# Eight conditioning products moved from TensorE to VectorE, the expert loop's head placed at a fixed slot, and each next loop bound read inside the body

## The chip, the cores and the metric

The kernel runs on one core of a Trainium2 chip. The metric is the device time of one execution in microseconds (us); lower is better. All arithmetic is fp32.

## The reference, cut to what matters

One layer over x of 256 tokens by 1024 columns, with a conditioning vector c:

```python
mod = silu(c) @ w_ada + b_ada                  # 6 x 1024: shift1, scale1, gate1, shift2, scale2, gate2
h = rms_norm(x, norm1_g) * (1 + scale1) + shift1
z = h @ w_in                                   # inputs of the convolution, q/kv latents, two branch gates
y_conv = zb * short_causal_conv(zc * zx)       # 8 channel tiles of 128
y_mla = mla_branch(...)                        # 8 heads, latent attention, rotary part of 64
x = x + gate1 * ((sig(zg_conv)*y_conv + sig(zg_mla)*y_mla) @ w_o)
h2 = rms_norm(x, norm2_g) * (1 + scale2) + shift2
for each token: top-1 group of 4, then top-2 of its 8 experts:
    out += weight * ((silu(h2 @ w_gate[e]) * (h2 @ w_up[e])) @ w_down[e])
x = x + gate2 * out
```

## The kernel before

Every engine has a queue written out by hand; they meet at counting semaphores. There is no planner.

**Setup and latents.** The columns of `w_ada` come in 12 items of 512 columns (`ada_d[n]`, 2 MB each: 8 row tiles `k` of 128 x 512). An item on TensorE (`ada_item`) is 8 x 4 matmuls: for each row tile `k` and each quarter `q`, silu(c) repeated over 32 columns (`c_rep`) is the stationary operand of column group `q`, and 128 columns of the weights stream past. In fp32 each matmul shows as two records, so an item is 64. Its result, 4 groups of 32 equal rows, is copied by ScalarE (`ada_copied`), transposed (L649, `ada_turned`) and added to the bias by VectorE (L950, `mod_ready`). Items 0 to 3 (shift1, scale1) are needed for the latents and run at the start. They are not touched.

**Heads.** A loop over 8 heads, unrolled, runs attention for head `h` and, woven into it, the convolution's projections for head `h + 1` and item `4 + h` of the modulation. TensorE's order in head `h`: q, k (`qk_ready`), attention output of head `h - 1`, tile 0 of the next head's projection (it waits for that head's weights, `ring_landed`), v (`v_ready`), sums of squares, tiles 1 and 2, scores (`s_ready`), **the item** (`ada_done`), tile 3, the item's transpose, tile 4, transposes of the probabilities. VectorE in head `h`: `q_x`, `q_n`, `merge(h - 1)`, the rotary products in even heads (L917, L919, L920), the reciprocal of the key norm (L922), `k_n`, `k_r`, `conv_taps(h + 1)`, the score maximum, the softmax's scaling, the bias add of the item (L950), `conv_gated(h + 1)` (L892, L893).

**SyncE's queue of transfers.** Weights of the heads go by turns into two slots of a ring (`mix_load`, 3.0 to 3.2 MB). `beside_load(j)` brings item `4 + j` into the head of expert place 3 (`ada_beside`). Experts 0 to 2 are loaded in heads 1 to 3. One queue holds, for each `c`: `mix_load(c + 2)` behind `v_ready` of head `c`, an expert, then `beside_load(c + 1)` behind `ada_done` of item `4 + c`. Experts 3 to 6 come from the end of the heads on.

**Experts.** Tokens are sorted into windows of 32 slots, each of one expert: here 35 windows for 32 experts. An expert's weights are 3 MB; there are 7 places. Expert `e + 7` is loaded into the place of expert `e` once the last window of `e` has finished (`down_ready`, in `next_expert`). TensorE runs an outer loop of 4 rounds over 7 unrolled places, and the last 4 experts unrolled behind it. For each expert an inner loop runs over its windows; its bounds are read from a table in SBUF (`windows_before`, a register load). A window is: gate and up products (32 matmuls), `gather` of the next window's rows (8), a transpose behind `gu_copied` (L770), `combine` (8), `turn_rows` of the next window (L744, L745), the down products (8).

Of the kernel before, what the change touches and what calls it, by code (L numbers as in the profile page):

```python
# [8 lines left out]
ALU = mybir.AluOpType  # L9
# [3 lines left out]
P = 128  # L13
D = 1024
T = 256
KT = D // P
TT = T // P
HEADS = 8
# [7 lines left out]
WIN = 32  # L26
# [44 lines left out]
def block_kernel(nc, xT_d, pos_d, small_d, const_d, ada_d, lat_d, mix_even_d, mix_odd_d, wo_d, ex_d, out_d):  # L71
    with ExitStack() as ctx:
# [3 lines left out]
        def sem(name):  # L76
            return ctx.enter_context(nc.semaphore(name))
# [103 lines left out]

        ada_beside = wex[:, OWN - 1, 0:ADA_COLS]
        ada_rows = wex[:, OWN - 1, GU_COLS:GU_COLS + P]

        def sm(name, i=0, n=None, parts=P):
            a, w = SMALL[name]
# [39 lines left out]
        w_tok_ready, slot_tok_ready, spread_ready, spread_copied = sem("w_tok_ready"), sem("slot_tok_ready"), sem("spread_ready"), sem("spread_copied")  # L226
        y_cleared = sem("y_cleared")
        ada_copied, ada_turned = sem("ada_copied"), sem("ada_turned")
        mod_ready = sem("mod_ready")

        xw_ready, gu_ready, gu_copied, gu_turned = sem("xw_ready"), sem("gu_ready"), sem("gu_copied"), sem("gu_turned")
# [18 lines left out]
        @block.sync  # L250
        def _(sp):
            sp.dma_start(xT[:], xT_d).then_inc(x_landed, 16)
            sp.dma_start(small[:], small_d).then_inc(small_landed, 16)

            def ada_load(n):

                sp.dma_start(wex[:, n, 0:ADA_COLS], ada_d[n]).then_inc(ada_landed[n], 16)  # L257

            def split_load(e, part):
                dst, cols = ((split_head, slice(0, GU_COLS // 2)), (split_tail, slice(GU_COLS // 2, GU_COLS + DOWN_COLS)))[part]  # L260
                sp.dma_start(dst, ex_d[e][:, cols]).then_inc(ex_landed[EX_SLOTS - 1], 16)

            def expert_load(s, e):
                if s < len(ex_place):
                    sp.dma_start(ex_place[s], ex_d[e]).then_inc(ex_landed[s], 16)
                else:
                    split_load(e, 0)
                    split_load(e, 1)

            def ring(n, src):  # L270

                if n == 2:
                    sp.wait_ge(lat_ready, 1)
                elif n > 2:
                    sp.wait_ge(v_ready, n - 2)
                sp.dma_start(ring_slot[n % 2][:, 0:src.shape[1]], src).then_inc(mix_landed[n % 2], 16)

            def mix_load(j):
                ring(MIX0 + j, (mix_even_d, mix_odd_d)[j % 2][j // 2])

            def lat_load(n):
                sp.dma_start(ring_slot[0][:, n * LAT_PART:(n + 1) * LAT_PART], lat_d[n]).then_inc(lat_landed[n], 16)  # L282

            ada_load(0)
            sp.dma_start(const[:], const_d).then_inc(const_landed, 16)
            ada_load(1)
            lat_load(0)
            sp.dma_start(posi, pos_d).then_inc(pos_landed, 16)
            lat_load(1)
            ada_load(2)  # L290
            lat_load(2)
            ada_load(3)
            lat_load(3)
            mix_load(0)

            def beside_load(j):
                sp.wait_ge(ada_done, 4 + j)
                sp.dma_start(ada_beside, ada_d[4 + j]).then_inc(ada_landed[3], 16)

            beside_load(0)  # L300
            mix_load(1)
            for c in range(HEADS):
                if c + 2 < HEADS:
                    mix_load(c + 2)
                else:
                    ring(WO0 + c + 2 - HEADS, wo_d[c + 2 - HEADS])
                if 1 <= c < OWN:
                    expert_load(c - 1, c - 1)
                if c + 1 < HEADS:
                    beside_load(c + 1)  # L310
            sp.wait_ge(ada_turned, 4 + HEADS)
            expert_load(OWN - 1, OWN - 1)
            last = EX_SLOTS - 1
            sp.wait_ge(merged_ready, HEADS)
            split_load(last, 1)
            for n in range(2):
                sp.wait_ge(wo_ready, 2 * n + 2)
                expert_load(OWN + n, OWN + n)
            sp.wait_ge(h2r_ready, 2)
            sp.wait_ge(lg_ready, 1)  # L320
            split_load(last, 0)
            sp.wait_ge(table_ready, 1)

            def next_expert(s, e):

                upto = windows_before(sp, e + 1)
                sp.wait_ge(down_ready, upto)
                expert_load(s, e + EX_SLOTS)

            for e in range(EXPERTS - EX_SLOTS):  # L330
                next_expert(e % EX_SLOTS, e)
            for m in range(KT):
                sp.wait_ge(out_done, m + 1)
                sp.dma_start(out_d[m], xT[:, m, :]).then_inc(out_stored, 16)
            sp.wait_ge(out_stored, 16 * KT)
# [138 lines left out]
        def _(pe):  # L474
# [3 lines left out]
            def ada_item(items, out):  # L478

                w = items.rearrange("p (k c) -> p k c", k=KT)  # L480
                for k in range(KT):
                    for q in range(4):
                        last = mm(out[q * WIN:(q + 1) * WIN, :], c_rep[:, k, :], w[:, k, q * P:(q + 1) * P], k == 0, k == KT - 1)
                return last
# [96 lines left out]
            for h in range(HEADS):  # L581
# [57 lines left out]
                mm(ps[:, 3, P:P + T], q_n[:, P:T], k_n, True, False)  # L639
                mm(ps[:, 3, P:P + T], q_r[rope, P:T], k_r[rope, :], False, True).then_inc(s_ready, 1)  # L640

                pe.wait_ge(ada_landed[3], 16 * h + 32)
                ada_item(ada_beside, ps[:, 0, 0:P]).then_inc(ada_done, 1)
                if h + 1 < HEADS:
                    conv_tile(h + 1, 3, ps[:, 6, T:2 * T]).then_inc(zbg_ready, 1)
                else:
# [86 lines left out]
            def gather(n):  # L733

                pe.wait_ge(sel_ready, n + 1)
                for t in range(TT):
                    for q in range(4):
                        last = mm(ps[q * WIN:(q + 1) * WIN, 3, 0:T], sel[:, t, :], h2_rows[:, t, q * T:(q + 1) * T], t == 0, t == TT - 1)
                last.then_inc(rows_ready, 1)
# [14 lines left out]
                                  False, True, skip_group_check=True)  # L754
                last.then_inc(combined, 1)

            def window(place, use, n):

                wdn = place_down(place).rearrange("p (f c) -> p f c", f=2)

                pe.wait_ge(ex_landed[place], use * (16 if place < len(ex_place) else 32))
                pe.wait_ge(xw_ready, n + 1)
                for k in range(KT):
                    for q in range(4):
                        last = mm(ps[q * WIN:(q + 1) * WIN, 0, 0:P], xw[:, k, :], place_gu(place, k)[:, q * P:(q + 1) * P], k == 0, k == KT - 1)
                last.then_inc(gu_ready, 1)
                gather(n + 1)

                pe.wait_ge(gu_copied, n + 1)
                nc.tensor.transpose(ps[:, 1, 0:P], gu_sb, ident).then_inc(gu_turned, 1)  # L770
                combine(n)
                turn_rows(n + 1)

                pe.wait_ge(act_done, n + 1)
                for f in range(2):
                    for q in range(4):
                        last = mm(ps[q * WIN:(q + 1) * WIN, 2, 0:T], act_t[:, f * WIN:(f + 1) * WIN], wdn[:, f, q * T:(q + 1) * T], f == 0, f == 1)
                last.then_inc(down_ready, 1)

            gather(0)  # L780
            spread(1, slot_tok)
# [1 line left out]
            pe.wait_ge(spread_copied, 2)  # L783
            pe.wait_ge(table_ready, 1)
            ROUNDS = EXPERTS // EX_SLOTS
            with pe.Fori(0, ROUNDS) as i:
                upto = windows_before(pe, i * EX_SLOTS)
                for s in range(EX_SLOTS):
                    at, upto = upto, windows_before(pe, i * EX_SLOTS + (s + 1))
                    with pe.Fori(at, upto) as n:  # L790
                        window(s, i + 1, n)
            upto = windows_before(pe, ROUNDS * EX_SLOTS)
            for e in range(ROUNDS * EX_SLOTS, EXPERTS):
                at, upto = upto, windows_before(pe, e + 1)
                with pe.Fori(at, upto) as n:
                    window(e % EX_SLOTS, ROUNDS + 1, n)
            combine(upto)


        @block.vector  # L800
        def _(dve):
# [93 lines left out]
            def merge(h):  # L895
# [4 lines left out]
                link(v.scalar_tensor_tensor(o_t, m_gate, 1.0, ps[:, 2, T:2 * T], ALU.add, ALU.mult))  # L900
                v.scalar_tensor_tensor(merged[:, h, :], o_t, 0.5, merged[:, h, :], ALU.mult, ALU.add).then_inc(merged_ready, 1)

            conv_taps(0)
            conv_gated(0)
            for h in range(HEADS):
                rope = slice(ROPE * (h % 2), ROPE * (h % 2 + 1))
                dve.wait_ge(sq_ready, h + 1)
# [7 lines left out]
                if h % 2 == 0:  # L915
                    dve.wait_ge(qx_ready, h // 2 + 1)
                    link(v.tensor_tensor(q_r, q_x, cos_t, ALU.mult))  # L917
                    dve.wait_ge(swap_ready, h // 2 + 1)
                    link(v.tensor_tensor(rope_t, sin_t, ps[:, 1, T:2 * T], ALU.mult))  # L919
                    link(v.tensor_tensor(q_r, q_r, rope_t, ALU.add))  # L920
                dve.wait_ge(rk_sqrt, h + 1)
                link(v.reciprocal(rk, rk_s))  # L922
                link(v.tensor_tensor(k_n, rk, ps[:, 0, T:2 * T], ALU.mult))
# [30 lines left out]
                    v.tensor_tensor(sm("b_router"), sm("b_router"), ps[:, 1, 0:36], ALU.add).then_inc(bias_ready, 1)  # L954
                if h + 1 < HEADS:
                    conv_gated(h + 1)
            merge(HEADS - 1)


# [228 lines left out]
```

## Time and profile before

| | |
|---|---|
| median of 3 runs | 537.12 us (532.66, 537.4, 537.12) |
| profiled execution: time / span | 537.62 us / 535.8 us |
| mean granted TensorE clock | 0.988 |
| busy: TensorE / VectorE / ScalarE / GpSimd | 499.5 / 183.6 / 148.1 / 153.2 us |
| moved by DMA | 161.94 MB, 302 GB/s over the span |

The span runs from the first to the last instruction; the remaining 1.8 us of the execution lie around it. The stages: start and latents to about 70 us, heads to about 307 us, router to about 321 us, experts to about 530 us, then the store.

### The profile page before, as it was taken

To read this page: it belongs to the slowest core of one execution; us is meant where nothing else is said; L and a number is where in the kernel's file an instruction comes from. 1 tells how busy PE (TensorE), PEld (TensorE's weight loads), DVE (VectorE), ACT (ScalarE), POOL (GpSimd) and SP (SyncE) were. 2 spreads that over 40 slices of the span, in tenths; PEclk is the share of its full clock that TensorE was granted. 3 is DMA by queue.
4 is the path that set the end of the run, shared out by engine and by line. 5 is a ranking of instruction groups with operands and counts; after the bars stand their busy time and mean duration, and the time that the engine had idled before them with its cause. 6 is when DMAs were issued, how large, how long until landed. Compare 5 with 4: busy or idle time off the path is not lost.

```text
span 535.8 us, 14859 instructions
## 1 busy us (share of the span) xinstructions
PE 499.5 (93%) x6205; PEld 388.9 (73%) x6206; DVE 183.6 (34%) x559; ACT 148.1 (28%) x276; POOL 153.2 (29%) x195
## 2 busy tenths in 40 slices
PE   4699999999999999999999969998999899899994
PEld 3587888888888888888888736765666566566663
DVE  0721624242524252424241442333233323233333
ACT  3012122322222232313131241323332242233221
POOL 0000010101010101010100005766676676677662
PEclk9989999999999999999999988999999999999999
DMA  8996417394959473624446973979999999999972
GB/s 356 414 435 248 178 32 276 125 428 192 417 222 413 183 270 146 254 122 158 157 158 247 393 302 145 369 309 432 425 431 435 429 428 435 428 429 435 425 329 80
DMA packets 10690, 161.94 MB, mean 302 GB/s; under 512 B 1185, under 2 KB 2465, under 8 KB 3105
## 3 DMA queue, kind: packets, MB, share of 16 engines
q1 hardware_dynamic: 10656, 161.45, 73.3%
q8 instruction: 27, 0.44, 0.3%
q14 instruction: 7, 0.05, 0.0%
HBM read 160.40 MB, written 1.05 MB: 301 GB/s over the span
## 4 chain that ended last, share of the span: by engine, by line
PE 83%; DMA 11%; issue 2%; DVE 1%; ACT 1%; SPq 1%; DVEq 0%; ACTq 0%
PE ps L476 79%; DMA wex<-in_ex 7%; DMA wex<-in_ada 4%; PE ps L744 1%; PE ps L770 1%; PE ps L745 1%; DVE xT L1068 1%; ACT act L449 0%; ACT L452 0%; SPq L282 0%; PE ps L662 0%; PE ps L664 0%; PE ps L663 0%; PE ps L649 0%; SPq L257 0%
## 5 line engine op out<-in xcount | busy, mean ns | idle before, releaser
L476 PE MATMUL ps<-act,wmix 128*128 128x256 f32 x864 | 194.6, 382 | 1.0 <-DVE act L850 1.0
L476 PEld LDWEIGHTS ps<-act,wmix 128*128 128x128 f32 x864 | 161.9, 190 | 24.9 <-issue 3.5
L357 POOL TENSOR_SCALAR work<-trig,work 128x256 f32<-128x256 f32 x70 | 65.0, 938 | 63.4 <-issue 54.2
L476 PE MATMUL ps<-wex,work 128*32 128x128 f32 (+1 forms) x1840 | 70.8, 301 | 11.1 <-issue 9.8
L343 POOL TENSOR_TENSOR work<-work,trig 64x256 f32<-64x256 f32 x8 | 5.8, 719 | 254.5 <-ACT work L410 152.9
L476 PE MATMUL ps<-work 32*128 32x256 f32 (+6 forms) x864 | 72.7, 374 | 0.6 <-ACT work L470 0.6
L476 PEld LDWEIGHTS ps<-wex,work 128*32 128x32 f32 x1840 | 50.3, 111 | 29.0 <-issue 14.3
L476 PEld LDWEIGHTS ps<-work 32*128 32x128 f32 (+3 forms) x864 | 47.5, 168 | 13.3 <-issue 3.3
L476 PE MATMUL ps<-act,work 128*32 128x256 f32 (+1 forms) x704 | 43.5, 367 | 2.5 <-DVE work L1035 1.3
L467 ACT ACT_TABLE_LOAD x35 | 44.9, 1283 | 1.0 <-issue 0.4
L361 POOL TENSOR_TENSOR work<-work,trig 128x512 f32<-128x512 f32 x35 | 44.7, 1277 | 0.0
L364 POOL TENSOR_TENSOR work<-work 128x256 f32<-128x256 f32 x35 | 25.5, 730 | 49.0 <-PE ps L476 49.0
L1053 DVE COPY work<-ps 128x128 f32<-128x128 f32 x35 | 10.2, 292 | 84.3 <-PE ps L476 84.3
L470 ACT COPY work<-ps 128x256 f32<-128x256 f32 x35 | 13.0, 373 | 84.1 <-PE ps L476 84.1
L476 PE MATMUL ps<-wmix,work 128*32 128x128 f32 (+2 forms) x704 | 32.6, 294 | 2.0 <-issue 2.0
L476 PEld LDWEIGHTS ps<-wmix,work 128*32 128x32 f32 (+1 forms) x704 | 25.3, 117 | 8.9 <-DVE work L1061 5.8
L476 PEld LDWEIGHTS ps<-act,work 128*32 128x32 f32 x704 | 22.3, 112 | 10.7 <-DVE work L1061 2.1
L476 PE MATMUL ps<-wex,c_rep 128*32 128x128 f32 x768 | 24.6, 282 | 4.4 <-DMA wex<-in_ada 4.4
L476 PEld LDWEIGHTS ps<-wex,c_rep 128*32 128x32 f32 x768 | 21.2, 113 | 8.2 <-DMA wex<-in_ada 5.0
L1061 DVE TENSOR_TENSOR work<-ps,mod 128x256 f32<-128x256 f32 x35 | 14.9, 425 | 33.9 <-PE ps L745 33.9
L467 ACT ACTIVATE work<-ps 128x64 f32<-128x64 f32 x35 | 7.8, 224 | 58.2 <-PE ps L770 58.2
L476 PE MATMUL ps<-work,wmix 128*128 128x256 f32 x104 | 23.8, 379 | 0.0
(181 smaller groups left out, 422.9 us busy)
## 6 DMA issues: line engine op xcount, KB each, us to landing
wex<-in_ex SPq DMA_DIRECT2D x20, 3072.0 KB, 18.5
wex<-in_ada SPq DMA_DIRECT2D x12, 2048.0 KB, 10.7
wmix<-in_ex SPq DMA_DIRECT2D x8, 3072.0 KB, 20.2
wmix<-in_mix_even SPq DMA_DIRECT2D x4, 3200.0 KB, 10.6
wmix<-in_mix_odd SPq DMA_DIRECT2D x4, 3008.0 KB, 10.8
work<-in_ex SPq DMA_DIRECT2D x4, 2048.0 KB, 19.8
wmix<-in_wo SPq DMA_DIRECT2D x2, 2048.0 KB, 8.2
act<-in_ex SPq DMA_DIRECT2D x4, 1024.0 KB, 16.5
```

What stands on the lines that cost most here:

```text
L343: nc.gpsimd.tensor_tensor(k_sq[0:ROPE, :], k_sq[0:ROPE, :], k_rope_sq[0:ROPE, :], ALU.add).then_inc(sq_joined, 1)
L357: nc.gpsimd.tensor_scalar(comb_both[:, rows], slot_row[:, rows], lane_now, None, ALU.is_equal).then_inc(comb_half, 1)
L361: nc.gpsimd.tensor_tensor(comb_both, comb_both, weight_row, ALU.mult).then_inc(comb_pair, 1)
L364: nc.gpsimd.tensor_tensor(comb, comb_both[:, 0:T], comb_both[:, T:2 * T], ALU.add).then_inc(comb_ready, 1)
L467: nc.scalar.activation(silu_t, ps[:, 1, 0:2 * WIN], ACT.Silu).then_inc(silu_done, 1)
L470: nc.scalar.copy(y_sb, ps[:, 2, 0:T]).then_inc(y_copied, 1)
L476: return nc.tensor.matmul(out, lhsT, rhs, start=start, stop=stop, **kw)
L744: nc.tensor.transpose(ps[:, 0, P:2 * P], rows_sb[:, 0:P], ident)
L745: nc.tensor.transpose(ps[:, 0, 2 * P:3 * P], rows_sb[:, P:T], ident).then_inc(rows_turned, 1)
L770: nc.tensor.transpose(ps[:, 1, 0:P], gu_sb, ident).then_inc(gu_turned, 1)
L1053: v.tensor_copy(gu_sb, ps[:, 0, 0:P]).then_inc(gu_copied, 1)
L1061: v.tensor_tensor(xw_v, xw_ps, shift2, ALU.add).then_inc(xw_ready, 1)
```

## The change

It has three parts.

**VectorE's modulation.** For items 4 to 11, VectorE now forms `ada_sum = sum over k of w[:, k, :] * c[k]` (128 x 512) in 8 instructions, each waiting for the one before: steps 0 to 4 of item `4 + h` right behind `conv_gated(h)`, steps 5 to 7 inside head `h`, behind L917 in even heads and behind `merge(h - 1)` in odd ones. TensorE then needs 4 matmuls (8 records) with a matrix of ones to sum over the partitions. `beside_load(j)` now waits for VectorE's sum of the item before (`ada_summed`) and stands ahead of `mix_load` in SyncE's queue.

**Aligned loop.** The outer expert loop's first instruction is put at slot 0 of a block of instructions.

**Bounds.** The upper bound of the next expert but one is read inside `window`, behind the gather, rather than between two experts. It is read again in each window of an expert.

```diff
+        ada_sum = wex[:, OWN - 1, GU_COLS + P:GU_COLS + P + ADA_TILES * P]
...
             def beside_load(j):
-                sp.wait_ge(ada_done, 4 + j)
+                if j == 0:
+                    sp.wait_ge(ada_done, 4)
+                else:
+                    sp.wait_ge(ada_summed, j)
                 sp.dma_start(ada_beside, ada_d[4 + j]).then_inc(ada_landed[3], 16)
...
             for c in range(HEADS):
+                if c + 1 < HEADS:
+                    beside_load(c + 1)
                 if c + 2 < HEADS:
                     mix_load(c + 2)
...
-                if c + 1 < HEADS:
-                    beside_load(c + 1)
...
-                pe.wait_ge(ada_landed[3], 16 * h + 32)
-                ada_item(ada_beside, ps[:, 0, 0:P]).then_inc(ada_done, 1)
+                pe.wait_ge(ada_summed, h + 1)
+                for q in range(4):
+                    last = mm(ps[q * WIN:(q + 1) * WIN, 0, 0:P], ones[:, 0:WIN], ada_sum[:, q * P:(q + 1) * P], True, True)
+                last.then_inc(ada_done, 1)
...
                 gather(n + 1)
+                later = windows_before(pe, following) if following is not None else None
...
-            with pe.Fori(0, ROUNDS) as i:
-                upto = windows_before(pe, i * EX_SLOTS)
+            with nc.Fori(0, ROUNDS, engines=[pe.engine], head_slot={pe.engine: 0}) as i:
+                at, upto = windows_before(pe, i * EX_SLOTS), windows_before(pe, i * EX_SLOTS + 1)
                 for s in range(EX_SLOTS):
-                    at, upto = upto, windows_before(pe, i * EX_SLOTS + (s + 1))
                     with pe.Fori(at, upto) as n:
-                        window(s, i + 1, n)
+                        later = window(s, i + 1, n, i * EX_SLOTS + (s + 2) if s + 1 < EX_SLOTS else None)
+                    at, upto = upto, later
...
+            def ada_steps(j, steps):
+
+                w = ada_beside.rearrange("p (k c) -> p k c", k=KT)
+                if steps[0] == 0:
+                    dve.wait_ge(ada_landed[3], 16 * j + 32)
+                    dve.wait_ge(ada_done, 4 + j)
+                for k in steps:
+                    if k == 0:
+                        link(v.tensor_scalar(ada_sum, w[:, k, :], c_rep[:, k, 0:1], None, ALU.mult))
+                    elif k < KT - 1:
+                        link(v.scalar_tensor_tensor(ada_sum, w[:, k, :], c_rep[:, k, 0:1], ada_sum, ALU.mult, ALU.add))
+                    else:
+                        v.scalar_tensor_tensor(ada_sum, w[:, k, :], c_rep[:, k, 0:1], ada_sum, ALU.mult, ALU.add).then_inc(ada_summed, 1)
+
             conv_taps(0)
             conv_gated(0)
+            ada_steps(0, range(0, 5))
             for h in range(HEADS):
...
                     link(v.tensor_tensor(q_r, q_x, cos_t, ALU.mult))
+                    ada_steps(h, range(5, KT))
                     dve.wait_ge(swap_ready, h // 2 + 1)
...
+                if h % 2 == 1:
+                    ada_steps(h, range(5, KT))
...
                     conv_gated(h + 1)
+                    ada_steps(h + 1, range(0, 5))
```

## Rows read from the trace of the kernel before

**Rows 1.** The page, part 1: busy us, share of the span, instructions.

```profile
PE 499.5 (93%) x6205; PEld 388.9 (73%) x6206; DVE 183.6 (34%) x559; ACT 148.1 (28%) x276; POOL 153.2 (29%) x195
```

**Rows 2.** The chain of waits in order of time: start us, us, what.

```profile
44.97 48.72 PE ps L476 x284
...
319.32 2.13 issue
...
464.04 35.34 DMA wex<-in_ex
...
522.33 2.82 PE ps L476 x80
```

**Rows 3.** Timeline of TensorE in head 4: start, us, engine, line, shapes, count, [idle before].

```profile
196.60 1.95 PE L476 MATMUL ps<-wex,c_rep 128*32 128x128 f32 x64
...
196.60 1.69 PEld L476 LDWEIGHTS ps<-wex,c_rep 128*32 128x32 f32 x64 [0.33 <-issue]
198.48 3.32 PEld L476 LDWEIGHTS ps<-act,wmix 128*128 128x128 f32 x16 [0.20 <-issue]
```

**Rows 4.** Timeline of VectorE in heads 4 and 5.

```profile
183.72 0.42 DVE L917 TENSOR_TENSOR work<-work,trig 128x256 f32<-128x256 f32 x1
...
187.98 0.42 DVE L919 TENSOR_TENSOR work<-trig,ps 128x256 f32<-128x256 f32 x1 [3.84 <-PE ps L476]
...
208.99 0.48 DVE L912 TENSOR_SCALAR work<-ps,work 128x256 f32<-128x256 f32 x1 [5.44 <-ACT work L407]
...
215.48 1.75 DVE L922 RECIPROCAL work<-work 128x256 f32<-128x256 f32 x1 [4.65 <-ACT work L420]
```

**Rows 5.** VectorE's groups with shapes kept apart: count | busy us, mean ns.

```profile
L886 DVE SCALAR_TENSOR_TENSOR work<-work,small 128x256 f32<-128x256 f32 x8 | 3.9, 484 | 0.3
L885 DVE TENSOR_SCALAR work<-work,small 128x256 f32<-128x256 f32 x8 | 2.8, 353 | 0.3
L838 DVE TENSOR_TENSOR act<-xT,work 128x2048 f32<-128x2048 f32 x1 | 2.3, 2292 | 0.0
```

**Rows 6.** Timeline in heads 4 and 5: a ring load's issue, the next slot's use.

```profile
186.59 0.33 SPq L276 DMA_DIRECT2D wmix<-in_mix_even  x1
...
208.64 3.33 PEld L476 LDWEIGHTS ps<-act,wmix 128*128 128x128 f32 x16
```

**Rows 7.** DMA issues at 186.59 and at 198.61 us: KB, us to landing.

```profile
wmix<-in_mix_even SPq DMA_DIRECT2D x1, 3200.0 KB, 10.7
...
wex<-in_ada SPq DMA_DIRECT2D x1, 2048.0 KB, 7.5
```

**Rows 8.** Timeline of TensorE in the experts.

```profile
339.14 2.82 PE L476 MATMUL ps<-wex,work 128*32 128x256 f32 x80
...
381.47 1.95 PE L476 MATMUL ps<-wex,work 128*32 128x128 f32 x64 [0.22 <-issue]
...
384.22 0.14 PEld L770 LDWEIGHTS ps<-const,work 128*128 128x128 f32 x1 [0.41 <-DVE work L1053]
...
387.21 1.69 PEld L476 LDWEIGHTS ps<-wex,work 128*32 128x32 f32 x64 [0.69 <-DVE work L1061]
...
458.46 1.96 PE L476 MATMUL ps<-wex,work 128*32 128x128 f32 x64 [1.37 <-issue]
```

**Rows 9.** Waits from 328 to 500 us: us in total, times, longest us.

```profile
PE ps L476 <- issue: 10.1, 27, 1.5
...
PE ps L476 <- DMA wex<-in_ex: 1.0, 1, 1.0
```

**Rows 10.** Timeline of SyncE's queue: the first and the last four loads into places 0 to 3.

```profile
328.70 28.30 SPq L265 DMA_DIRECT2D wex<-in_ex  x4
...
464.04 17.59 SPq L265 DMA_DIRECT2D wex<-in_ex  x4
```

**Rows 11.** DMA issues at 356.67 and at 481.30 us: KB, us to landing.

```profile
wex<-in_ex SPq DMA_DIRECT2D x1, 3072.0 KB, 11.0
...
wex<-in_ex SPq DMA_DIRECT2D x1, 3072.0 KB, 40.8
```

More of the change, by code:

```diff
@@ L228, in block_kernel @@
         ada_copied, ada_turned = sem("ada_copied"), sem("ada_turned")
+        ada_summed = sem("ada_summed")
         mod_ready = sem("mod_ready")
@@ L755, in combine, with window @@
                 last.then_inc(combined, 1)
-            def window(place, use, n):
+            def window(place, use, n, following):
                 wdn = place_down(place).rearrange("p (f c) -> p f c", f=2)
@@ L778, in window @@
                 last.then_inc(down_ready, 1)
+                return later
             gather(0)
@@ L785, in _ @@
             ROUNDS = EXPERTS // EX_SLOTS
-            with pe.Fori(0, ROUNDS) as i:
-                upto = windows_before(pe, i * EX_SLOTS)
+            with nc.Fori(0, ROUNDS, engines=[pe.engine], head_slot={pe.engine: 0}) as i:
+                at, upto = windows_before(pe, i * EX_SLOTS), windows_before(pe, i * EX_SLOTS + 1)
                 for s in range(EX_SLOTS):
-                    at, upto = upto, windows_before(pe, i * EX_SLOTS + (s + 1))
                     with pe.Fori(at, upto) as n:
-                        window(s, i + 1, n)
-            upto = windows_before(pe, ROUNDS * EX_SLOTS)
+                        later = window(s, i + 1, n, i * EX_SLOTS + (s + 2) if s + 1 < EX_SLOTS else None)
+                    at, upto = upto, later
+            at, upto = windows_before(pe, ROUNDS * EX_SLOTS), windows_before(pe, ROUNDS * EX_SLOTS + 1)
             for e in range(ROUNDS * EX_SLOTS, EXPERTS):
-                at, upto = upto, windows_before(pe, e + 1)
                 with pe.Fori(at, upto) as n:
-                    window(e % EX_SLOTS, ROUNDS + 1, n)
-            combine(upto)
+                    later = window(e % EX_SLOTS, ROUNDS + 1, n, e + 2 if e + 1 < EXPERTS else None)
+                at, upto = upto, later
+            combine(at)
         @block.vector
```

## The prediction, made before the result was known

> **What bounds the kernel now.** I read the page first: TensorE is busy for 499.5 of 535.8 us [rows 1]. Such a share says neither where it is the limit nor what comes next, so I read the chain of waits in order of time. From 44.97 us through all heads the chain is TensorE's own matmuls, one row behind the other, with no wait for another engine [rows 2]; a microsecond of matmul that leaves a head leaves the whole. Between 307 and 319 us lies the router, small steps on several engines, then 2.13 us in which TensorE waits for nothing that the trace shows, just before the expert loop. In the experts the chain is TensorE again, until it jumps at 499.38 us to a load of 35.34 us [rows 2]: a load that had long been queued. TensorE itself waited only 1.0 us for it [rows 9].
>
> So the experts have two limits almost at the same height. *The load stream.* Four loads into places 0 to 3 are issued from 328.70 to 357.0, the last at 356.67 (the start of the last issue, 0.33 before the end of that row) [rows 10]. That one, of expert 10, meets an idle queue: it takes 11.0 us [rows 11]. The last is issued at 481.30 and lands 40.8 us later, at 522.1 [rows 10, 11]. Between them are 21 landings in 522.1 - 367.7 = 154.4 us, 7.35 us each, with the queue never empty. The last window begins at 522.33 [rows 2]: the end hangs on a stream that starts with the end of expert 3. *TensorE.* One window follows another after 5.74 us, of which 0.22 is idle between two experts [rows 8]; 5.52 of it is work and fixed switches. Between two windows of one expert there is no such gap: the down products and the next gate products run through as 80 records [rows 8].
>
> **VectorE's modulation, on TensorE.** An item's 64 records start at 196.60, and the next weight load starts at 198.48: 1.88 us [rows 3]. The weight loads come 1.69 / 64 = 0.026 us apart, so the 64th matmul starts 1.66 us in and, ending at 1.95, lasts 0.29; the next shape's load begins 0.07 before that end. With 8 records the last starts 7 x 0.026 = 0.18 us in: 0.18 + 0.29 - 0.07 = 0.40 us. The saving is 1.48 us an item, and 8 x 1.48 = 11.8 us. Bounds: in pure proportion 7/8 of 1.88, 1.65 an item, 13.2 in all; or 0.2 us more of unseen gap an item (the row's own 0.20), 1.3, 10.4 in all. The rows show 0.33 us in front of the item's weight loads and 0.20 behind them [rows 3]; the Trainium skill (TensorEngine Tiling (Array Packing), Key Properties) says that a change of tiling mode drains the engine. By a saving in proportion it would be 13.2 us; by that rule the two drains stay, and the trace agrees.
>
> **The same, on VectorE.** A step on 256 columns takes 0.484 us with a scalar and a second tensor, 0.353 with a scalar alone; 2048 columns take 2.29 us, 1.12 ns a column with all overhead [rows 5]. The 256 more columns thus cost at most 0.29: 0.77 and 0.64 us, and about 0.04 for each wait on the step before. Steps 0 to 4 are 0.68 + 4 x 0.81 = 3.9 us, steps 5 to 7 2.4 us. Steps 0 to 4 start where `conv_gated` ends, in front of idle time of 5.44 us in odd heads (208.99), more in even ones [rows 4]: 1.5 us to spare. Steps 5 to 7 stand in front of 3.84 us (even, before L919) and 4.65 us (odd, before L922) [rows 4]: 1.4 and 2.2 to spare. TensorE asks for the sum at 196.6, some 10 us after it is there. I cost all of it at nothing. Without this cover (VectorE at twice the rate per step) an odd head would lose 7.8 - 5.4 = 2.4 us, less what TensorE has queued.
>
> **The same, on SyncE's queue.** `beside_load` now waits for VectorE instead of TensorE and moves ahead of `mix_load` and, in heads 1 to 3, of an expert's load; both stand behind its wait and its 2 MB. In an even head the sum is there at 184.1 + 2.4 = 186.5, when the ring load was issued anyway, 186.59 [rows 4, 6]. Alone the item takes 7.5 us, the ring load 10.7 [rows 7]: 18.2 us even if they overlap in nothing, from 186.6 to 204.8. The slot is used at 208.64 [rows 6], 1.5 us earlier by the shorter head, so 2.3 us remain. The expert behind it is needed only after 300 us. GpSimd's queue does not change. Cost: nothing.
>
> **The bounds of the loop.** Taken out: the 0.22 us gap between two experts [rows 8]. Put in: one register load in each of 35 windows, behind the gather; behind it on TensorE's queue stand L770, `combine` and all that follows, and ScalarE and VectorE wait for L770. Its cover is the 0.41 us in which the weight load of L770 waits anyway [rows 8]. No row shows a load by itself. Where it stands today the weight loads pause for 0.69 us [rows 8], with two branches in it, so a load in the body adds x between 0 and 0.69 - 0.41 = 0.28 us a window. I take 0.15, the middle, since an unknown part of the 0.69 is the loop's. What counts before the stream of loads runs: three changes of expert gone (-0.7) and six windows with x: +0.9; together +0.2 (-0.7 to +1.0). The Trainium skill (DMA: Bandwidth & Descriptors, Latency and other measured facts) puts a floor of about 600 ns under a `tensor_load`; an estimate from it is x = 0.6 - 0.41 = 0.19, 0.2 us more in the time. No run here shows such a load alone.
>
> Later on, TensorE has room. From 321.45 (319.32 + 2.13) to the end of the last window, 522.33 + 5.52 = 527.9, it took 206.4 us for 35 windows [rows 2], of which 10.1 us were such gaps and 1.0 the wait for the load [rows 9]: 195.3 without. Three returns to the loop's head remain, 1.37 against 0.22 us [rows 8]: 3.5 us. So it needs 198.8 + 35x, and the load stream gives it 522.1 + 5.5 - 321.45 = 206.1. As long as x is below 7.3 / 35 = 0.21, the stream decides; at 0.28 TensorE decides and is 2.5 us late.
>
> **The aligned loop.** It adds a jump into the loop. Bound: a return to the head costs 1.15 us more than a plain change of expert [rows 8]. Below nothing: the 2.13 us of the entry [rows 2] could shrink to 1.37, 0.8 less. I take +0.2. Its effect on later rounds falls under the stream of loads.
>
> **The sum.** -11.8 (heads) + 0.2 (first experts) + 0.2 (entry) - 0.1 (the last window can start at the landing, 522.1) = -11.5 from the profiled 537.62: 526.1. The median of the three runs lies 0.5 lower, so 525.6.
>
> **Rivals.** (1) *The load in the body makes TensorE the limit.* x of 0.28 to 0.55 instead of 0.15: at 0.28 +2.5, about 528; at 0.55, 198.8 + 19.3 = 218.1 against 206.1, so 12.0 us and with them the whole gain are gone: 537. For it: nothing shows that TensorE's queue reaches over the load. Against: L770 waits anyway. (2) *VectorE or the ring takes part of the heads' gain back.* If a step took 1.1 us rather than 0.8, steps 0 to 4 would reach past the 5.44 us and `merge`, which v waits for, would slip. At 1.3 us a step the overrun is 1.1 us an odd head, some 4 us: 530. Against it: [rows 4, 5]. (3) *Slower: each window pays the load in full.* If the load does not start before the gather has drained and the queue must fill again behind it, the price is the pause of 0.69 plus the 0.41 that no longer overlaps, 1.1 us: 198.8 + 38.5 = 237.3 against 206.1, +31.2 - 11.8 = +19.4: 556. It decides from x = 0.21, and makes the kernel over 1% slower from 0.70. Against it: branches of the inner loop cost nothing visible [rows 8], so the queue does run ahead. (4) *The parts on the loop do nothing and the entry gets dearer by 1.15:* 527, inside the range.
>
> **How the numbers follow.** The forecast has 0.74 with (4) in it; (1) 0.12; (2) 0.09; (3) 0.05. Low end: -13.2 - 0.7 - 0.8 - 0.2 = -14.9, 522.2, and the runs of the kernel before lie up to 4.5 us under their median, of which I grant 1.5: 520.7. High end: -10.4 + 1.0 + 1.15 + 2.5 = -5.75, 531.4; I go to 530, which takes in most of (2) and the lower part of (1) and leaves the rest out. Over 1% faster is below 531.7: the forecast, (2) and a part of (1), 0.86. Within 1%, 0.09; slower by over 1%, 0.05. A measurement of this kernel tells about 1% from no change.
>
> **What would show it.** Right: 8 records of an item in under 0.5 us; heads over about 12 us earlier; VectorE's 128x512 steps at 0.65 to 0.8 us and no wait of TensorE for them; no 0.22 us gap between experts; TensorE waiting longer for loads than the 1.0 us now; the last landing about 12 us before 522. Wrong: a weight load of L770 later than 0.41 us behind the gather in each window, no wait for loads at the end (TensorE decides), waits for `ring_landed` in the heads, or single returns of over 1 us inside an expert of two windows, from where a block of the aligned loop begins.

## The result, and the profile after

The changed kernel takes 520.49 us (519.96 to 520.67), the kernel before 534.89 in the same comparison (532.52 to 537.4): a ratio of 0.9728, 95% interval 0.9668 to 0.9789. The forecast was 525.6; its range ended at 520.7, 0.2 us above the measured time. The profiled execution has a span of 518.8 us against 535.8. Here and below a time is the median of all runs of a kernel, while ratios and their intervals use its fast runs alone, those within 1.5% of its fastest.

The chain of waits of the changed kernel, in order of time (start us, us, what):

```profile
43.20 47.19 PE ps L481 x228
...
303.75 2.52 issue
306.27 4.44 PE ps L481 x80
...
440.58 42.81 DMA wex<-in_ex
483.51 2.82 PE ps L481 x80
```

Beside [rows 2]: the heads begin 1.8 us earlier (43.20 against 44.97), the expert loop 15.2 us earlier (306.27 against 321.45), and the jump to a load that had long been queued is still there, at 483.39 against 499.38. TensorE's timeline in head 4, beside [rows 3]:

```profile
188.72 0.16 PEld L481 LDWEIGHTS ps<-wex,ones 128*32 128x32 f32 x8 [0.33 <-issue]
188.72 0.43 PE L481 MATMUL ps<-wex,ones 128*32 128x128 f32 x8
...
189.07 3.32 PEld L481 LDWEIGHTS ps<-act,wmix 128*128 128x128 f32 x16 [0.20 <-issue]
```

From the item's first weight load to the next shape's it is 0.35 us instead of 1.88, with the same pauses of 0.33 and 0.20 around it: 1.53 us an item, 12.2 in eight. VectorE's timeline around it, beside [rows 4]:

```profile
193.71 0.42 DVE L902 SCALAR_TENSOR_TENSOR act<-work 128x256 f32<-128x256 f32 x1
194.05 0.48 DVE L920 TENSOR_SCALAR wex<-wex,c_rep 128x512 f32<-128x512 f32 x1
194.56 3.11 DVE L922 SCALAR_TENSOR_TENSOR wex<-wex,c_rep 128x512 f32<-128x512 f32 x4
...
200.62 0.79 DVE L910 SCALAR_TENSOR_TENSOR act<-work,act 128x256 f32<-128x256 f32 x1
201.34 1.52 DVE L922 SCALAR_TENSOR_TENSOR wex<-wex,c_rep 128x512 f32<-128x512 f32 x2
202.90 0.75 DVE L924 SCALAR_TENSOR_TENSOR wex<-wex,c_rep 128x512 f32<-128x512 f32 x1
...
203.68 0.33 SPq L303 DMA_DIRECT2D wex<-in_ada  x1
```

Steps 0 to 4 take 3.62 us, from 194.05 to 197.67, in front of work that begins near 199.7. The item's load is issued as soon as the sum is there. Now an expert window, TensorE's timeline and the waits from 306 to 484 us, beside [rows 8, 9]:

```profile
364.49 1.05 PE L481 MATMUL ps<-act,work 128*32 128x256 f32 x16
...
365.46 0.14 PEld L778 LDWEIGHTS ps<-const,work 128*128 128x128 f32 x1 [0.41 <-DVE work L1081]
```

```profile
PE ps L481 <- issue: 7.2, 4, 3.0
PE ps L481 <- DMA wex<-in_ex: 4.7, 3, 1.8
PE ps L481 <- DMA wmix<-in_ex: 3.6, 2, 1.8
PE ps L481 <- DMA work<-in_ex: 1.8, 1, 1.8
```

The weight load behind the gather (L778; it was L770 in the kernel before) pauses 0.41 us as before, with the register read in front of it. Of the 27 short pauses between experts in [rows 9] three are left, the returns to the loop's head, 4.2 us together; the fourth of this row, 3.0 us, is the entry into the loop. In place of the others TensorE waits 10.1 us for loads, 6 times. The last load and its landing, by SyncE's queue and the issue at 459.81 us:

```profile
440.58 19.55 SPq L267 DMA_DIRECT2D wex<-in_ex  x4
```

```profile
wex<-in_ex SPq DMA_DIRECT2D x1, 3072.0 KB, 45.5
```

The last weights land at 459.8 + 45.5 = 505.3, 16.8 us before those of the kernel before; the end follows 13.5 us later (13.7 before).

### The profile page after: what moved, and what is told of

Same layout as the page of the kernel before. It is cut to its first block, busy times and chain, and to the rows that moved or that the text cites. A ratio compares the mean times of both kernels' runs of the same rounds, so it can differ in the third digit from the quotient of the medians.

```text
span 518.8 us, 14050 instructions
## 1 busy us (share of the span) xinstructions
PE 481.0 (93%) x5757; PEld 376.7 (73%) x5758; DVE 228.1 (44%) x623; ACT 148.1 (29%) x276; POOL 153.1 (29%) x195
## 4 chain that ended last, share of the span: by engine, by line
PE 82%; DMA 13%; issue 2%; DVE 1%; ACT 1%; SPq 1%; DVEq 0%; ACTq 0%
PE ps L481 78%; DMA wex<-in_ex 8%; DMA wex<-in_ada 4%; PE ps L751 1%; PE ps L778 1%; PE ps L752 1%; DVE xT L1096 1%; ACT act L454 0%; ACT L457 0%; SPq L284 0%; PE ps L669 0%; PE ps L670 0%; PE ps L656 0%; PE ps L671 0%; SPq L259 0%
## 5 line engine op out<-in xcount | busy, mean ns | idle before, releaser
L481 PE MATMUL ps<-wex,work 128*32 128x128 f32 (+1 forms) x1840 | 67.6, 298 | 11.9 <-issue 7.2
L922 DVE SCALAR_TENSOR_TENSOR wex<-wex,c_rep 128x512 f32<-128x512 f32 x48 | 36.0, 750 | 1.6
L1084 DVE COPY work<-ps 128x256 f32<-128x256 f32 x35 | 14.9, 424 | 20.8 <-PE ps L481 20.8
## 6 DMA issues: line engine op xcount, KB each, us to landing
wmix<-in_mix_even SPq DMA_DIRECT2D x4, 3200.0 KB, 15.6
wmix<-in_mix_odd SPq DMA_DIRECT2D x4, 3008.0 KB, 14.4
```

Source lines behind the costliest of these rows:

```text
L481: return nc.tensor.matmul(out, lhsT, rhs, start=start, stop=stop, **kw)
L922: link(v.scalar_tensor_tensor(ada_sum, w[:, k, :], c_rep[:, k, 0:1], ada_sum, ALU.mult, ALU.add))
L1084: v.tensor_copy(rows_sb, ps[:, 3, 0:T]).then_inc(rows_copied, 1)
```

## The experiments

Three theories stood against each other. **A:** the heads give 12.2 us, the bounds 1.3 to 1.6 where the load stream doesn't cover them, the fixed slot nothing; the rest of the profiles' 17.0 us is spread of the kernel before. **B:** part of it comes from the fixed slot. **C:** the read in the body costs what it saves. Each expectation below names its own A and B; a letter behind a result means the expectation just above it. The kernel before was measured again beside each group and took 534.0 to 534.6 us, so times of different groups compare to about 1 us.

**The kernel before, unchanged.**

> The kernel before, unchanged. Theory A (the profile of before was taken in its longer variant: 1.7 us lost in the start and 1.6 us in the step before the expert loop): the runs fall into two groups, near 532.5 and near 537.2, and a profile from the lower group shows the latents' second item at 7.3 instead of 9.0 us. Theory B (these 3 us are the change's): all profiles of this kernel show both losses. Ratio 1.000 either way.

Measured: 534.38 us against 534.62, ratio 0.9999 (0.9976 to 1.0022). The runs fill the stretch from 532.5 to 537.6 without falling into two groups; the rest of A is there. Its chain:

```profile
27.41 7.33 PE ps L476 x88
34.85 7.26 PE ps L476 x88
43.21 48.72 PE ps L476 x284
```

With a span of 531.9 us it lacks both losses that the profile of the forecast had: 1.8 us before the heads, where the first of these pieces took 8.96 us at a mean granted clock of 0.93 (from 20 to 45 us), and 1.6 us in the products just before the expert loop. Against this profile the change is worth 13.1 us.

**VectorE's modulation alone**, on the kernel before, with the new order of the transfers; the loop and its bounds as before.

> The kernel before with VectorE's modulation and the new order of SyncE's queue alone. Theory A: 8 x 1.53 = 12.2 us faster, experts' windows still 5.74 us apart, nothing else. Theory B (part of the rest also comes from here, by the transfers that arrive earlier): more than 13 us faster.

Measured: 575.72 us, ratio 1.0715 (1.0654 to 1.0777), 41 us *slower* than before. Neither theory. The heads are as short as in the changed kernel; so the loss in the expert loop is some 53 us. Its chain of waits there:

```profile
360.10 7.31 issue
...
368.90 2.85 issue
...
418.34 8.33 issue
...
428.15 3.12 issue
...
478.92 7.26 issue
```

Behind each of the three returns to the loop's head TensorE pauses for 7 to 8 us and then for 2 to 3, and waits for nothing that the trace shows. From 306 us on such waits are 53.4 us, against 12.9 in the kernel before. The other 13 us were not taken apart; the granted clock averaged 0.92 from 307 to 566 us, and 0.69 from 418 to 440 around the second pair of pauses, against 0.99 in the changed kernel's loop. The page of the same kernel, DMA queues (packets, MB):

```profile
q8 instruction: 51, 0.84, 0.6%
```

For the changed kernel this row reads 24 packets, 0.39 MB: 16 KB each. The 27 more make 9 for each of three returns to the loop's head. So the loop's code is fetched again in every round. That the fetches are slow because they queue with the weights is likely, since the weights' queue kept the DMA engines 96% busy from 358 to 367 us, but no run tests it. The modulation takes 448 matmuls and 448 weight loads out of the code ahead of the loop, 896 instructions, so the loop stands elsewhere. The Trainium skill (Advanced Engine Details and Errata, ISA Cache) gives TensorE 128 KB for code in lines of 16 KB, 256 instructions; the packets agree with the size of a line, and 896 is three and a half of them. An estimate from the page, 128 KB over 16 KB: 8 lines. The same section of the Trainium skill also says that there are only two lines. The changed kernel's trace does not agree with two: it goes round a loop of some 1,700 instructions, nearly seven lines, with 24 packets in all and none between 380 and 460 us, where two of its three returns lie.

**The two parts on the loop, each alone on the kernel before**, and **the changed kernel without the slot.**

```diff
 # slot_only, on the kernel before
-            with pe.Fori(0, ROUNDS) as i:
+            with nc.Fori(0, ROUNDS, engines=[pe.engine], head_slot={pe.engine: 0}) as i:
 # no_slot, on the changed kernel: the same line, the other way round
```

> The kernel before with the bounds read in the body alone. Theory A (only what shortens the six windows up to the load of expert 10 counts; the load stream hides the rest): windows 5.31 us apart, 1.3 to 1.6 us faster. Theory B (the whole of 28 changes of expert by 0.43 us counts): 12 us faster. Theory C (the read costs what it saves): no change.

> The kernel before with the outer expert loop's head at slot 0 alone. Theory A: the entry costs 0 to 1.2 us more, nothing else; ratio 1.000 to 1.002. Theory B (the slot takes away waits for code): returns to the head below 1.37 us and the step before the loop shorter, 1 to 3 us faster.

> The changed kernel without the fixed slot: VectorE's modulation and the bounds in the body. Theory A (the slot does nothing or costs the entry): as fast as the changed kernel or up to 1 us faster, ratio 0.972 to 0.974. Theory B (the slot is worth what the forecast missed): 2 to 3 us slower than the changed kernel, 0.978.

| kernel | us | ratio to before | 95% interval |
|---|---|---|---|
| bounds alone | 533.76 | 0.9976 | 0.9954 to 0.9997 |
| slot alone | 535.49 | 1.0011 | 0.999 to 1.0032 |
| changed, no slot | 565.74 | 1.0543 | 1.0501 to 1.0586 |

Bounds: A, 1.3 us by the ratio, with an interval from 0.2 to 2.5. Slot alone: A, nothing. The changed kernel without its slot: neither; it loses 45 us, far beyond what B meant, and shows 51 instruction packets like the kernel above. The slot is worth nothing where the loop already stood well, and decides everything once the code ahead has changed.

**Where may the head stand?** The changed kernel at slots 64, 104 and 144, the kernel before at slot 144, and a shorter loop.

> The kernel before with the outer expert loop's head at slot 144, nothing else. The loop is some 1,700 instructions long: a slot of 0 to some 90 lets it begin and end within 7 blocks of 256, a later one takes 8. Theory A (the slow runs of VectorE's modulation alone come from the place of the loop, which its shorter code ahead had shifted): 35 to 45 us slower, single pauses of several us on TensorE in each round, about 27 more instruction packets. Theory B (they come from the modulation itself): no change.

> The changed kernel with its loop's head at slot 64 in place of 0. Theory A (what counts is that the loop stays within 7 blocks: 64 + 1700 < 1792): as fast as the changed kernel, 520.5 us. Theory B (only a head at a block's start is fast): slower by several us.

> The changed kernel with its loop's head at slot 104. Theory A (104 + 1700 = 1804 is past 1792, the loop touches an eighth block): near 565 us, as without the fixed slot. Theory B (the loss grows with the distance from a block's start): a little slower than at 64.

> The changed kernel with its loop's head at slot 144. Theory A (the place of the loop in the code decides, whichever kernel it is in): 550 to 570 us, more than 24 instruction packets, pauses of several us. Theory B (the slow runs belong to kernels without the bounds in the body or without the modulation): 520.5 us.

```diff
 # short_slot144, in window()
-                for k in range(KT):
+                kts = 2 if place == EX_SLOTS - 1 else KT
+                for k in range(kts):
```

> As the one with its head at slot 144, but the windows in the last of the seven places do only the first 2 of 8 row tiles of their gate and up products (24 matmuls, 96 instructions, left out; those experts' results are partial). The head is where it was, the loop ends at slot 144 + 1604 = 1748, within 7 blocks. Theory A (the number of blocks that the loop reaches into decides): fast again, 517 to 521 us, 24 packets. Theory B (the head's slot decides): as slow as the one without the cut, 550 us or more.

| kernel, head's slot | us | instruction packets |
|---|---|---|
| changed, 0 | 520.49 | 24 |
| changed, 64 | 520.47 | 24 |
| changed, 104 | 521.77 | 24 |
| changed, 144 | 534.42 | 34 |
| changed, 144, loop 96 instructions shorter | 521.2 | 24 |
| before, no slot given | 534.62 | 27 |
| before, 0 | 535.49 | 28 |
| before, 144 | 560.08 | 37 |

The kernel before at slot 144 in its third round, TensorE's timeline:

```profile
411.11 1.07 PE L476 MATMUL ps<-work 128*32 128x256 f32 x16
420.27 3.19 PE L476 MATMUL ps<-wex,work 128*32 128x128 f32 x50 [8.09 <-issue]
424.81 0.53 PE L476 MATMUL ps<-wex,work 128*32 128x128 f32 x11 [1.35 <-issue]
```

The changed kernel at slot 144, its chain and its page:

```profile
401.87 7.14 issue
```

```profile
q8 instruction: 34, 0.56, 0.4%
```

So the place alone makes either kernel slow, with the modulation or without. The pair at slot 144 settles which place: the same head with a loop that ends 96 instructions sooner is fast. It is not that less work hides the loss: its trace has no long pause, the longest wait of this kind being the 3.1 us of the entry. It is the end of the loop that must not reach too far, not the head that must stand at a block's start. My figure for the edge is off: I count the loop at 1,700 instructions, which at slot 104 ends at 1804, 12 past the seventh block, and yet is fast. The edge lies between ends of 1804 and 1844 by my count; whether the count or the rule is off by these few stays open.

The expectations for slot 144 missed the size: they had 27 more packets and pauses in each round, 35 to 45 us in the kernel before and 550 to 570 us for the changed one. The traces show 10 more packets, and the long pause behind the second of the three returns only (8.09 and 7.14 us), where the kernels without a slot and with the modulation have 27 more and a long pause behind each. That slot 144 costs 14 us in the changed kernel and 26 in the one before goes with the 10.1 us that the changed kernel otherwise waits for loads: at slot 144 these waits are gone. Why only one return is hit stays open; the losses also spread within a kernel (530.7 to 547.9 in the changed one).

**The bounds with the slot kept.** The changed kernel with its bounds read between experts:

> The changed kernel with the bounds read between the experts as before: VectorE's modulation and the fixed slot. Theory A: the change's gain less what the bounds bring where they are not hidden by the load stream, 1.2 to 1.6 us: about 522. Theory B (the stream of loads hides the bounds wholly): 520.5.

Measured: 523.8 us, 0.9813 (0.9788 to 0.9837), 3.3 us behind the changed kernel, and as far behind the one at slot 64 (520.47), which ran beside it. More than A's 1.6, though the profiled spans differ by 1.9 (520.7 against 518.8). B is out.

**The load stream out of the way.**

```diff
 # light_after, on the changed kernel (without the down weights; the last place does the same in two parts)
+            def light_load(s, e):
+                if s < len(ex_place):
+                    sp.dma_start(ex_place[s][:, 0:GU_COLS], ex_d[e][:, 0:GU_COLS]).then_inc(ex_landed[s], 16)
...
-                expert_load(s, e + EX_SLOTS)
+                light_load(s, e + EX_SLOTS)
 # light_two, besides
                 later = windows_before(pe, following) if following is not None else None
+                again = windows_before(pe, following) if following is not None else None
```

> The changed kernel whose loads from expert 7 on leave out the down weights (2 MB in place of 3; those experts compute with stale down weights). Theory A (the load stream sets the end): TensorE's waits for loads, some 11.5 us, vanish and the time falls to about 509 us. Theory B (TensorE sets the end): no change from 520.5.

> As the one with light loads, but the bounds are read between two experts as before. With the stream out of the way the gap between experts shows in full: theory A, 0.43 us at some 28 changes of expert, 12 us slower than the light one with bounds in the body; theory B (a change of expert costs only the 0.22 us of idle time), 6 us slower.

> As the one with light loads, with a second register read behind the first in every window whose expert is followed by another in the unrolled code. Theory A (a read in the body is hidden while TensorE works through its queue): under 1 us slower than with one. Theory B (a read costs 0.15 to 0.28 us): 5 to 9 us slower.

Measured: 509.95, 522.26 and 516.71 us. The stream does set the end of the changed kernel: without it 10.5 us go. With it out of the way the bounds between experts cost 12.3 us, 0.44 at each of some 28 changes of expert (A), so the stream hides most of what this part saves. A second read is not free: it costs 6.8 us (B). The weight load behind the gather shows it, in the kernel with two reads:

```profile
367.92 0.14 PEld L786 LDWEIGHTS ps<-const,work 128*128 128x128 f32 x1 [0.65 <-DVE work L1089]
367.93 0.33 PE L786 MATMUL ps<-const,work 128*128 128x128 f32 x1 [0.17 <-issue]
```

0.65 us here (0.62 in the next window) against 0.41 with one read or none: the first fits into a pause that is there anyway, the second adds 0.24, and 6.8 us over some 28 windows is 0.24 too.

**The room on VectorE and in the ring.**

```diff
 # dve_double, in ada_steps
                 for k in steps:
+                    link(v.scalar_tensor_tensor(ada_more, w[:, k, :], c_rep[:, k, 0:1], w[:, k, :], ALU.mult, ALU.add))
 # ring_old, in SyncE's loop: the item's load back behind the others
-                if c + 1 < HEADS:
-                    beside_load(c + 1)
                 if c + 2 < HEADS:
                     mix_load(c + 2)
...
                     expert_load(c - 1, c - 1)
+                if c + 1 < HEADS:
+                    beside_load(c + 1)
```

> The changed kernel with a second 128x512 step in front of each of VectorE's steps, its result unused. Steps 0 to 4 become 7.8 us against some 5.4 us of room in odd heads. Theory A (the forecast's sizes): 1 to 2.5 us an odd head less what TensorE has queued, 3 to 10 us in all over the changed kernel. Theory B (VectorE has far more room than that): under 1 us.

> The changed kernel with the item's load behind the ring's and the expert's load in SyncE's queue, as before. Theory A (both orders have room: the item is asked for 20 us after its issue): no change, within 0.5 us of the changed kernel. Theory B (the new order is needed, since VectorE now asks for the item earlier than TensorE did): in heads 1 to 3 the item lands 22 us after issue, VectorE waits some 2 to 4 us there, 3 us or more slower.

Measured: 524.87 us for doubled steps, 4.4 over the changed kernel, as A has it: TensorE stands for 0.8 us in each of the four odd heads, waiting for `merge`, and nowhere else in the heads: 3.3 of the 4.4 us; the rest is not traced. And 536.6 us (ratio 1.0045, 1.0021 to 1.007) for the old order of transfers: it takes the whole gain back and 2 us more. B, and worse than B's "3 us or more". The chain and TensorE's timeline of that kernel:

```profile
132.82 23.20 DMA wex<-in_ada
156.05 0.50 DVE wex L920
```

```profile
161.18 1.22 PE L481 MATMUL ps<-wmix,work 128*128 128x128 f32 x4 [4.43 <-DVE act L910]
```

Behind a ring load and an expert the item lands 23.2 us after its issue. VectorE, which now asks for it at the end of the head, stands 8.1 us before step 0; steps 0 to 4 then push `merge` back, and TensorE, which needs it before v, stands for 3.25, 4.43 and 2.25 us. The stops are 9.9 of the 15.6 us between this profile and the changed kernel's. Two of them cost more than themselves. The windows behind the second and the third (the columns before the last three are busy times; then granted clock, DMA share, GB/s):

```profile
161.00:176.00 15.00, 14.82 (x66) 12.32 (x67) 7.60 (x17) 4.57 (x8) 0.00 (x0) 0.80 0.82 330
...
192.00:205.00 13.00, 12.46 (x68) 10.35 (x69) 9.11 (x21) 4.59 (x8) 0.00 (x0) 1.00 0.80 324
```

The mean granted clock is 0.80, a mixture of the two levels, behind the stop of 4.43 us, 0.90 (130 to 145 us) behind that of 3.25, and full behind that of 2.25; in the changed kernel it is 1.00 from 43 to 293 us.

## Why the prediction was off

**Right: the chain, the direction, the heads' term.** "VectorE's modulation, on TensorE" gave 11.8 us and it is 12.2: the drains at both changes of shape stay, as the rows had them, and 8 records take 0.35 us, not 0.40. A saving in proportion would have been 13.2.

**Right: the cover on VectorE.** Steps 0 to 4 were put at 3.9 us and take 3.6: the first, with a scalar alone, 0.48 us instead of 0.64, the others 0.75 instead of 0.77. The way in which rival 2 would have cost time is real: with doubled steps `merge` slips in odd heads and TensorE stands, 0.8 us each, where the forecast allowed up to 2.4.

**Right by luck: SyncE's queue.** The step put the new order at nothing, which holds: a ring load behind the item landed 16.3 us after its issue, where 18.2 were allowed. But the order was treated as a burden to be excused (two loads moved behind a wait). That the new order is what makes the modulation possible at all was not asked; left as it was it costs 16 us.

**The step that failed: "The bounds of the loop".** It took the gap of 0.22 us for the price of a change of expert, and x = 0.15 for the read; together +0.2 us before the load stream begins. But the row it cites beside it, 80 records run through in one piece between two windows of one expert, says more. The same point in these two windows of the kernel before:

```profile
337.44 0.33 PE L770 MATMUL ps<-const,work 128*128 128x128 f32 x1
...
342.75 0.33 PE L770 MATMUL ps<-const,work 128*128 128x128 f32 x1
```

They lie 5.31 us apart, not 5.52. A change of expert costs 0.43 us, and x is 0: neither the 0.15 nor the 0.19 estimated beside it. Half of the 0.43 is not idle time of TensorE's matmuls; that it is the lead of the weight loads, lost behind the pause, is my reading and was not tested. From the first window to the load of expert 10 it is 33.8 us now (340.06 - 306.27) against 35.2: -1.4 instead of +0.2. The same error stood in the balance of the two limits: where the light loads leave the end to TensorE, it needs about 194 us from the first window to the last (306.40 to 500.20), not 198.8 + 35x. So the stream decides by some 10 us, and rival 1 was never near.

**The aligned loop, a wrong question.** The step gave +0.2; between profiles in which the products ahead of the loop are equally fast, the way from the router to the first window grew by 0.36. But "its effect on later rounds falls under the stream of loads" and rival 4, "the parts on the loop do nothing", looked only at what the slot adds. Removing 896 instructions ahead of a loop was taken for free. It isn't: without the slot the same change is 5% slower than before, not 3% faster. No case of the forecast contained that, and it is the one thing in this change on which its sign hangs.

**The base.** Of the 5.1 us by which the forecast missed, 2.2 are its base: 537.12 was the median of three runs of a kernel that runs from 532.5 to 538.1, and 534.89 when measured again. The other 2.9 are the gain, put at 11.5 us and 14.4 by those medians. Between the two profiles without losses ahead of the heads and of the loop it is 13.1: the start and the heads 12.2, the expert loop to the end 1.2, less 0.4 for the entry. So 1.6 of the 2.9 are sizes of terms (0.4 in the heads, 1.2 to 1.3 in the loop, -0.2 at the entry). The last 1.3 are no part of either profile; against the later runs of the kernel before (534.1 us) 0.5 of them remain. They are not traced. The forecast saw that its base spread and granted 1.5 us for it in its low end; 2.2 were needed.

## What to carry to other kernels

Code is a resource with a place. Before instructions are taken out ahead of a long loop, ask where the loop ends in blocks of code, fix its place, and look at the count of instruction packets in the profile: 24 against 51 went with 45 us here. A transfer whose consumer moves earlier must move earlier in its queue too. And read the price of a pause off the whole distance between two equal pieces of work with and without it (5.74 against 5.31 us), not off the idle time alone (0.22).

## What the runs showed of the hardware that I had not expected

- A loop of some 1,700 TensorE instructions that ends too far in its blocks of code fetches them again: behind one of three returns at slot 144 (10 packets of 16 KB more), behind all three in the two kernels with the modulation and no slot (27 more). TensorE then pauses for 7 to 8 us at a return, and the time varies by up to 17 us from run to run of one kernel.
- One register read from SBUF behind 8 matmuls costs TensorE nothing; a second one, 0.24 us.
- In otherwise dense matmuls the granted clock averaged 0.90 and 0.80 over the 15 us behind stops of 3.25 and 4.43 us, and stayed full behind one of 2.25 (13 us).
